# Fused two-block network on one core: the passing operands of the split float32 products move to 64 bytes below the weights, modulo 512

## Time and profile before

| | us |
|---|---|
| median of 3 runs | 2449.75 (2447.69 to 2451.53) |
| the profiled execution | 2447.19 |
| its span | 2445.4 |
| PE busy, share | 2371.1, 97% |
| PE weight loads (PEld) busy | 2124.7, 87% |
| DVE busy | 1769.0, 72% |
| ACT busy | 1165.0, 48% |
| POOL busy | 148.7, 6% |

### The profile page before, as it was taken

One profiled execution on the slowest core, in us unless ns is written; L12 is line 12 of the kernel. 1 busy time (PEld: TensorE's weight loads), 2 busy tenths in 40 slices (PEclk: granted clock), 3 DMA queues, 4 the chain that ended last, 5 costly groups with the idle time before them and its releaser, 6 DMA issues. The chain is left out here.

```text
span 2445.4 us, 37022 instructions
## 1 busy us (share of the span) xinstructions
PE 2371.1 (97%) x14412; PEld 2124.7 (87%) x14412; DVE 1769.0 (72%) x2947; ACT 1165.0 (48%) x1715; POOL 148.7 (6%) x205
## 2 busy tenths in 40 slices
PE   5989999999999999999999999999999999999998
PEld 5889898888888888889899888888888888998998
DVE  7989887676767676678978676566767566655665
ACT  4542355444545454564145544455545523545544
POOL 0000352000000000000055000000000000000000
PEclk9989999999999999999999999999999999999999
DMA  9365435786666666434534686665555523343553
GB/s 357 141 228 164 147 130 165 270 292 241 232 240 232 240 232 223 149 110 148 178 120 138 203 309 210 212 207 189 189 189 189 189 79 105 129 148 135 184 189 104
DMA packets 133556, 460.66 MB, mean 188 GB/s; under 512 B 15152, under 2 KB 16432, under 8 KB 132912
## 3 DMA queue, kind: packets, MB, share of 16 engines
q1 hardware_dynamic: 133424, 458.90, 55.0%
HBM read 445.73 MB, written 13.11 MB: 188 GB/s over the span
## 5 line engine op out<-in xcount | busy, mean ns | idle before, releaser
L1691 DVE TENSOR_TENSOR ring_lo<-ring,ring_hi 128x1024 fp32r<-128x1024 f32 x421 | 507.0, 1223 | 86.1 <-ACT ring_hi L1594 86.1
L1594 ACT ACTIVATE ring_hi<-ring 128x1024 fp32r<-128x1024 f32 x421 | 434.9, 1053 | 132.4 <-PE banks L346 119.4
L319 PE MATMUL banks<-normed_lo,ring_hi 128*128 128x512 f32 x1344 | 477.9, 398 | 0.0
L344 PE MATMUL banks<-ring_hi,work_lo 128*128 128x512 f32 x1024 | 400.4, 391 | 6.5 <-PEq L1187 3.7
L345 PE MATMUL banks<-ring_lo,work_lo 128*128 128x512 f32 x1024 | 399.9, 391 | 0.0
L346 PE MATMUL banks<-ring_hi,work_lo 128*128 128x512 f32 x1024 | 399.1, 390 | 0.0
L320 PE MATMUL banks<-normed_lo,ring_lo 128*128 128x256 f32 x1344 | 377.2, 281 | 0.0
L319 PEld LDWEIGHTS banks<-normed_lo,ring_hi 128*128 128x128 f32 x1344 | 252.5, 188 | 61.7
L361 DVE TENSOR_TENSOR ring_lo<-ring,ring_hi 128x1024 fp32r<-128x1024 f32 x185 | 225.0, 1223 | 73.3 <-ACT ring_hi L356 72.8
L320 PEld LDWEIGHTS banks<-normed_lo,ring_lo 128*128 128x128 f32 x1344 | 253.8, 189 | 3.3
L356 ACT ACTIVATE ring_hi<-ring 128x1024 fp32r<-128x1024 f32 x185 | 194.8, 1055 | 94.2 <-PE banks L311 53.5
(11 more groups left out here) (401 smaller groups left out, 4396.4 us busy)
## 6 DMA issues: line engine op xcount, KB each, us to landing
ring<-wstream SPq DMA_DIRECT2D x716, 512.0 KB, 3.5
arena<-wstream SPq DMA_DIRECT2D x96, 512.0 KB, 5.3
spill<-one_hots SPq DMA_DIRECT2D x44, 256.0 KB, 4.2
rstd<-spill SPq DMA_DIRECT2D x16, 256.0 KB, 3.7
pool_and_keys<-spill SPq DMA_DIRECT2D x14, 256.0 KB, 3.8
routes<-spill SPq DMA_DIRECT2D x14, 256.0 KB, 4.6
residual<-xT SPq DMA_DIRECT2D x1, 1024.0 KB, 8.2
arena<-mixconst SPq DMA_DIRECT2D x2, 512.0 KB, 4.9
```

Source lines behind the costliest of these rows:

```text
L319: pe.matmul(dst, w_hi[:, o], HR[:, k, :], start=(k == 0), stop=(k == KD - 1), skip_group_check=True)
L344: pe.matmul(dst, hi[:, t], w_hi[:, o], start=first, stop=False)
L1594: sc.activation(RING_HI[:, u % HIGHS, :], RING[:, u % SLOTS, :], ACT.Copy)\
L1691: dve.tensor_tensor(RING_LO[:, u % SLOTS, :], RING[:, u % SLOTS, :], RING_HI[:, u % HIGHS, :].bitcast(F32), ALU.subtract).then_inc(S("spli ...
```

## The change

Only addresses change. In `program`, layer_vectors and modulation are allocated ahead of normed instead of behind consts_sb, with a padding tile before and one behind normed. `Arena.passing()` moves the next piece to 112 floats (448 bytes) modulo 128 floats (512 bytes), and five stages call it ahead of the piece that passes. The numbers of bytes in the paddings are 32 and 64.

```diff
@@ program
         RING, RING_LO = two("ring", [P, SLOTS, D])
+        LVS = sb("layer_vectors", [P, DEPTH, L_COLS])
+        MOD = sb("modulation", [P, 48])
+        sb("pad_normed", [P, 8])
         HF, HR = two("normed", [P, KD, 2 * T])
+        sb("pad_work", [P, 16])
         H, H_LO, H_HI = HF[:, :, T:2 * T], HR[:, :, T:2 * T], HR[:, :, 0:T]
         WK, WK_LO = two("work", [P, 2, D])
...
         CST = sb("consts_sb", [P, C_COLS])
-        LVS = sb("layer_vectors", [P, DEPTH, L_COLS])
         PK = sb("pool_and_keys", [P, 512])
-        MOD = sb("modulation", [P, 48])
...
@@ class Arena
+            def passing(self):
+
+                self.at += (112 - self.at) % 128
...
@@ mixer of a layer
             PL = a(2, T)
+            a.passing()
             MIX, MIX_LO, MIX_HI = a.split(8, T)
...
```

## The result

The changed kernel takes 2440.64 us (median of 8 runs, 2437.34 to 2445.47) against 2451.34 for the kernel before (8 runs on the same chips, 2447.69 to 2456.3): ratio 0.9947, 95% interval 0.9935 to 0.9959. The forecast was 2415 with a range of 2402 to 2434. The direction holds; of the 35 us that were forecast, 10.7 came.

A forecast was written before the change was run, and what follows sets the result against it. TensorE, busy 97% of the span, was taken as the bound: time is matmul count times start-to-start pitch. Seven terms summed to 35.0 us saved, from a median of 2449.75 to 2415 us, range 2402 to 2434.

The forecast's parts named there:

- term 1, the pairs: Expert stage, 1344 pairs of a 512- and a 256-wide matmul: 352.5 to 344 ns each, saving 11.4 us.
- the pairs don't gain: Rival, expert stage: the conflict of a 512-wide stream is not at its start; 2426 us in all, chance 0.18.
- Term 2: Feed-forward stage, 41 units of 24 matmuls and a group of 72: 6.0 ns less each, saving 6.3 us.
- Terms 3, 5, 6: Experts' query projection saves 4.6 us, both layers' input projection 2.0, experts looked at ahead 5.0, by quicker matmuls.
- Terms 7 and 4: Arena operands (384 matmuls of MIX, 576 others) save 4.5 us; cross attention's queries (192 matmuls) save 1.2 us.
- Plain float32 products at 0: 352 products of normed (L1932): no row at another address, 2.4 us either way possible, taken as 0.
- The rule of independent ports: Skill's rule for moving operand and weight load: address could not matter, saving 0; kept as a rival, not the forecast.
- the no-change rival: Rival: F is quick because one operand passes eight times in a row, not by address; 2449.75 us, chance 0.06.

The follow-up runs named there:

- 512-only sweep: TensorE alone, network not computed: chains of 24 matmuls of 512 columns, operand offsets 0 to 252 bytes; 226.7 ns each at 0, 233.3 at 192.
- first triples version: Changed kernel with each 512- and 256-column pair as three 256-column matmuls, high weights loaded twice: 2432.27 us, ratio 0.9912 to the kernel before.
- The sweeps: TensorE alone, network not computed: chains like the network's at operand offsets in steps of 16 or 4 bytes; 256-column products at 120 ns at 0, 113.3 at 112.
- that with triples and normed at 112 modulo 256: Changed kernel with pairs as three 256-column matmuls (high weights loaded twice) and normed at 368 bytes modulo 512 instead of 448: 2423.24 us, ratio 0.987.

## Why the prediction was wrong

- **Step that failed: term 1, the pairs.** "I take 344, nearer the floor, since the rest of a 512-wide matmul runs with no weight load beside it" gave 11.4 us, and the pairs moved from 352.5 to 353.1. By the table this is 12.5 us of the gap, the largest part. The mistake was to put together a pair from two floors, one of which (226.5) was read where moving and stationary operands lie at offset 0, and the other (113.3) 64 bytes below. The 512-only sweep shows that each was the floor of its own place: 226.7 at 0 and 233.3 at 192, where 256 columns are at 120.0 and 113.3. With the floors of one place the sum is 346.6 at 192, so that explains half of the 13 ns between 340 and 353. The other half is the alternation itself, which no sum of the two chains gives (352.5 against 346.7 at 0, 343.3 against 346.5 at 28); why, no run shows. The rival "the pairs don't gain" said this (0.18), and its reason, "offset 0 is not bad by itself there", was the right reading of the earlier trace rows. But its number for the whole, 2426, was far too low as well, since the other terms were sized too large.
- **Term 2 (feed-forward, 6.3 us): right.** 6.1 us by the same trace, pitch 113.3 as read from F. That all 48 matmuls of each cycle settle at 113.3 and none at 117.7 could not be known from the rows; it was luck in part.
- **Terms 3, 5, 6: right in kind, sized too large.** At 448 a chain has two stable pitches, and in the network a good part of the chains takes 117.7 (28 of the 92 products of normed, 18 of the 28 of the arena, half of the look-ahead's runs of nine; the averages are 114.8 for products of normed and 116.4 for the look-ahead). The prediction took 113.3 from one unit of F; two of the 22 units of F in the same trace were at 117.7. Query projection 3.75 of 4.6, look-ahead 3.3 of 5.0; the stretches with the two input projections came out 0.2 us longer together, where 2.0 less was forecast; their steps wait for other engines.
- **Terms 7 and 4, arena operands and cross attention's queries: 3.4 us of 5.7.** Same cause: the five units of the second block's output projection and the eight with MN all took 117.8, those of the first block's MIX and of OX some 113.3 and some 117.8. Alone the arena's operands gave 4 us with normed left at 0.
- **Plain float32 products at 0:** the state-space stretch grew by 0.65 us, and that is the clock, not the address: 4.7 us of it ran at 1.2 GHz instead of 3.4. In the first triples version, with normed at 448 too and 3.4 us at 1.2 GHz, it took 127.3 us as before. Taking the address at 0 was right.
- **Not in the sum:** 3.5 us at the first v units, by the clock behind an old wait. It comes and goes from version to version, and it went against the change in the profiled execution. By the medians the change brought 10.7 us, by the profiled ones 9.3.
- **The rule of independent ports.** The Trainium skill, page "TensorE: Matmul & The Clock Gate", section "Step-by-step: what each phase is for", has the weight load take nothing from the running matmul. The sweeps, with no other engine at work, have 113.3 to 124.5 ns for the same chain by address alone, and the v units show that moving the weights does the same as moving the operand. So these float32r chains do not agree with the rule, and the no-change rival fell. How the two reads get in each other's way no run shows.
- **The period** was taken as 512 bytes, after the width of the weight blocks; it is 256. No number of the forecast hung on it.

## What to carry to other kernels

Read the pitch of a full TensorE from start times per chain, look for more than one value in it, and sweep the operand's offset with the very chain (widths and order) that the kernel has: a good place for one rhythm is no evidence for another. Prefer a place whose good pitch came back on every pass over one that is sometimes as good. A chain can also be fitted to the place: here three matmuls of 256 columns at 112 modulo 256 beat 512 and 256 at 448 by 11 ns of 353, although the weights are loaded once more. Pairs at 28 or 60, at 343 in the sweep, were not tried in the network and may do as well.

## What the runs showed of the hardware

- With float32r operands, no chain of 256 columns at granted clock 1.00 settled below 113.3 ns from start to start, and none of 512 columns below 226.5; a plain float32 matmul of the same 256 columns took 216 with normed at 0 and at 448 (median of L1932's, L1941 after).
- The pitch depends on the distance between passing operand and weights modulo 256 bytes, in places of 4 bytes: from 113.3 to 124.5 for 256 columns, 226.6 to 240 for 512, 343 (at 28 and 60) to 363 (once, at 244) for the pair.
- Several places have two stable pitches (113.3 and 117.8 at 192), kept for a whole chain once it has settled, chosen by how it starts: ten starts at 448 gave nine times 113.3 and once 117.8.
- The cheapest version measured was that with triples and normed at 112 modulo 256: 2423.24 us, 1.3% under the kernel before and 0.7% under the changed one by the medians.
